# Three steps of a chunked linear-attention recurrence moved by one half group among the projection matmuls

## The reference, cut to what matters

```python
def step(carry, inp):                       # one chunk of tokens, all heads
    c_s, n_s, m = carry
    ...
    s = jnp.einsum('bhtd,bhsd->bhts', qc, kc) * jnp.exp(dmat - m_t[..., None])
    num = (w_inter[..., None] * jnp.einsum('bhtd,bhde->bhte', qc, c_s)
           + jnp.einsum('bhts,bhse->bhte', s, vc))
    ...
    h_out = num / jnp.maximum(jnp.abs(den), jnp.exp(-m_t))[..., None]
    ...
    c_new = decay[..., None, None] * c_s + jnp.einsum('bhs,bhsd,bhse->bhde', wk, kc, vc)
```

## Time and profile before

| what | us |
|---|---|
| median of 3 runs | 2176.84 (2175.14 to 2182.24) |
| the profiled execution, as timed | 2182.6 |
| its span in the trace | 2180.9 |
| late projections with the recurrence, in the trace | 119 to 367 |
| first matmuls after the barrier | from 369.79 |

### The profile page before, as it was taken

One profiled execution on the slowest core, in us unless ns is written; L12 is line 12 of the kernel. 1 busy time (PEld: TensorE's weight loads), 2 busy tenths in 40 slices (PEclk: granted clock), 3 DMA queues, 4 the chain that ended last, 5 costly groups with the idle time before them and its releaser, 6 DMA issues.

```text
span 2180.9 us, 39001 instructions
## 1 busy us (share of the span) xinstructions
PE 2104.2 (96%) x11205; PEld 1814.9 (83%) x11206; DVE 1597.7 (73%) x2121; ACT 1274.1 (58%) x1631; POOL 911.1 (42%) x909
## 2 busy tenths in 40 slices
PE   7999999999997999999999999999999999999996
PEld 6877777865886998888998899899887899889895
DVE  4555662553337778898878987888998888898876
ACT  4245342545235667676666766666776766776664
POOL 2015762244564234445334533433546443543532
PEclk9999998799996999999999999999999999999998
DMA  5233455303245779899877987987999987998976
GB/s 187 76 92 109 138 141 143 101 1 103 86 147 197 258 261 356 271 383 388 272 260 255 375 295 262 349 270 258 369 384 376 389 282 260 362 388 289 357 260 213
DMA packets 290264, 543.26 MB, mean 249 GB/s; under 512 B 39400, under 2 KB 51653, under 8 KB 290212
## 3 DMA queue, kind: packets, MB, share of 16 engines
q1 hardware_dynamic: 267972, 486.17, 66.1%
q0 software_dynamic: 22240, 56.42, 6.9%
HBM read 509.34 MB, written 44.14 MB: 254 GB/s over the span
## 4 chain that ended last, share of the span: by engine, by line
PE 75%; DVE 2%; DMA 2%; issue 2%; ACT 1%; POOL 0%; SPq 0%; DVEq 0%; POOLq 0%; ACTq 0%
PE banks L2634 17%; PE banks L208 11%; PE banks L210 11%; PE banks L209 11%; PE banks L2636 7%; PE banks L2011 3%; PE banks L2570 2%; PE banks L2569 2%; PE banks L1295 2%; DMA RAW<-in_expert_w_gate_up 1%; PE banks L2633 1%; PE banks L1997 1%; PE banks L1996 1%; DVE VL L1274 1%; PE banks L1973 1%
## 5 line engine op out<-in xcount | busy, mean ns | idle before, releaser
L1274 DVE TENSOR_TENSOR VL<-RAW,VH 128x2048 fp32r<-128x2048 f32 x389 | 882.2, 2287 | 28.8 <-ACT VH L1269 23.2
L1269 ACT ACTIVATE VH<-RAW 128x2048 fp32r<-128x2048 f32 x390 | 733.7, 1910 | 111.6 <-PE banks L210 76.3
L2634 PE MATMUL banks<-T,VH 128*128 128x384 f32 x1920 | 542.1, 357 | 2.5 <-DVE T L1315 2.5
L2636 PE MATMUL banks<-T,VL 128*128 128x192 f32 x1680 | 422.1, 251 | 0.0
L2634 PEld LDWEIGHTS banks<-T,VH 128*128 128x128 f32 x1920 | 345.8, 190 | 3.4 <-issue 2.9
L2636 PEld LDWEIGHTS banks<-T,VL 128*128 128x128 f32 x1680 | 321.6, 191 | 0.5
L2329 POOL DMA_INDIRECT out<-yb,ycur x32 | 78.3, 2447 | 413.0 <-DVE yb L2473 395.8
L209 PE MATMUL banks<-VL,T 128*128 128x512 f32 x544 | 211.9, 390 | 0.0
L208 PE MATMUL banks<-VH,T 128*128 128x512 f32 x544 | 211.9, 390 | 0.0
L210 PE MATMUL banks<-VH,T 128*128 128x512 f32 x544 | 211.8, 389 | 0.0
L208 PE MATMUL banks<-VH,A 128*128 128x512 f32 x512 | 204.1, 399 | 4.5 <-DVE A L2453 3.3
(11 more groups left out here) (391 smaller groups left out, 4070.1 us busy)
## 6 DMA issues: line engine op xcount, KB each, us to landing
RAW<-in_expert_w_gate_up SPq DMA_DIRECT2D x528, 512.0 KB
RAW<-in_expert_w_down SPq DMA_DIRECT2D x262, 512.0 KB
RW<-in_w_in SPq DMA_DIRECT2D x24, 512.0 KB, 5.8
xin<-in_x SPq DMA_DIRECT2D x8, 512.0 KB, 11.4
MBC<-dM SPq DMA_DIRECT2D x8, 512.0 KB, 11.1
dQ<-parts SPq DMA_DIRECT2D x8, 512.0 KB, 3.0
dK<-parts SPq DMA_DIRECT2D x8, 512.0 KB, 3.0
WRAW<-in_w_out SPq DMA_DIRECT2D x8, 512.0 KB, 8.3
```

The costliest lines, as they stand in the source:

```text
L1269: act.activation(VH[:, i, ks], RAW[:, i, ks], ACT.Copy).then_inc(s_hi, 1)
L1274: dve.tensor_tensor(VL[:, i, ks], RAW[:, i, ks], VH[:, i, ks].bitcast(f32), ALU.subtract).then_inc(s_w, 1)
L2634: last = pe.matmul(o[:, 0:2 * NW], VH[:, c % 3, k, col], T2[:, k], start=k == 0, stop=k == KT - 1)
L2636: pe.matmul(o[:, HI_ALL], VL[:, c % 3, k, col], T2[:, k, HI_ALL], start=False, stop=False)
```

## The change

On PE, `keys` goes from slot 1 to slot 0 and `update` from slot 5 to slot 6. On DVE, `quotient` goes from slot 6 to slot 5 and `state` from slot 5 to slot 6. ACT, POOL and SP keep their programs. No instruction is added or removed.

```diff
@@ DVE, piece
                         if s == 4:
                             numerator(t)
                         if s == 5:
+                            quotient(t)
+                        if s == 6:
                             state(t)
-                        if s == 6:
-                            quotient(t)
@@ PE, piece
                     elif t < TT:
-                        if s == 1:
+                        if s == 0:
                             keys(t)
                         if s == 2:
                             from_state(t)
                             scores(t)
                         if s == 4:
                             from_chunk(t)
-                        if s == 5:
+                        if s == 6:
                             update(t)
```

## The result

The changed kernel takes 2186.11 us (median of 12 runs, 2183.84 to 2191.68), the kernel before, timed beside it, 2180.63 (12 runs). The ratio is 1.003, 95% interval 1.0019 to 1.004: slower by 4.1 to 8.7 us; the medians differ by 5.5. Forecast were 7.6 us, 1.0035.

What follows compares the result with a forecast made beforehand. PE was taken to bound the kernel, with DVE's queue ahead of state now stopping it. Steps +6.0 us, quotient 0 and clock +1.6 gave +7.6 on 2176.84, so 2184.4 us, range 2176.5 to 2190.

Steps and rivals of the forecast that it cites:

- Step 0: Keys 0 wait 2.9 us for the gate factors; PE 0.4 us later at the state's read, lower end -1.4.
- Step 1: The numerator's wait of 1.84 us goes, keys 2 wait 1.4 us behind DVE's weight parts; net -0.5 us.
- Step 2: DVE's sums of group q3 stand ahead of the state, keys 3 wait 0.3 us; net +0.1 us.
- Step 3: Last group of q: state behind normed and two weight parts, keys 4 wait 8.6 us; +4.1 us, the dearest.
- Step 4: State behind the rest of k0, held by ACT's rounding and a store; keys 5 wait 3.3 us, net +1.8.
- the ruler: PE's stretch lengths from the earlier profile: half 2.72 us, update 0.90 more, keys to state's read 2.95, on to from_chunk 8.05.
- Step 5: State behind normed of k5, keys 6 wait 3.4 us, waits for v's weights (2.2) go; net -1.0 us.
- Step 6: State behind the rest of k7, held by a late store; keys 7 wait 2.9 us; net +1.1 us.
- The clock term: PE's stands of about 3 us bring one fall to half clock: +1.6 us, range 0 to 5.4.
- stores land on their own: Rival: late stores land soon after issue, so two DVE waits and the clock loss go; +0.1 us, 2176.9, chance 0.09.
- lost time is absorbed: Rival: DVE is the real pace and lost time is found again; +1 us, 2178, chance 0.07.
- worse: Rival: every PE stand brings half clock and two quotients are held 1.9 us each; +15.2 us, 2192.0, chance 0.08.

Runs made afterwards that it cites:

- c: Changed kernel, but DVE calls state in slot 5 right behind the quotient and stands there until PE's update; ratio to the kernel before 0.9996.
- a: Kernel before with only PE's keys moved from slot 1 to slot 0; ratio to the kernel before 1.0005.
- d: Changed kernel with DVE's quotient moved from slot 5 to slot 6, behind state; ratio to the kernel before 1.0055.
- e: Changed kernel with PE's keys back in slot 1 and DVE standing at state in slot 5; 2178.75 us against 2181.91 before, ratio 0.9975.
- f: Kernel before with DVE's first two weight parts ahead of normed in a projection's last group; ratio to the kernel before 0.9983.
- g: Kernel e with DVE's first two weight parts ahead of normed in a projection's last group; total ratio 0.998.

## Why the prediction was right, and where it was not

The mechanism held: c, which differs from the changed kernel only in what DVE has queued ahead of the state, gets all of the 7.9 us back, so half a group is enough in sum and the loss was the queue. By steps, each against the same place before, the stage's later start of 0.75 us taken off:

*Step 0.* Stand 2.58 (forecast 2.9), read of the state 0.6 later (0.4). Then the clock: 1.00 from 136 to 144, so by the next step PE was 1.1 ahead. I had taken the fall, and it did not come; my lower end, -1.4, was nearly met.

*Step 1.* Net -0.6 (-0.5), wait 0.97 (1.4). *Step 2.* +0.3 (+0.1).

*Step 3.* Wait 8.30 (8.6), `state` behind the two weight parts as forecast; net +3.4 (+4.1). From keys to read 7.19 us, of which 1.5 is the clock (2.1 forecast).

*Step 4.* Wait 2.96 (3.3). Net +3.3 instead of +1.8, because the clock fell: keys to read took 281.22 - 273.85 = 7.37 where the ruler says 5.67.

*Step 5.* Wait 3.71 (3.4). The waits for the weights of `v` went, as forecast, but to `from_chunk` 6 the net is +2.1 instead of -1.0: keys to read took 8.19, 2.5 of it clock.

*Step 6.* Wait 2.56 (2.9), no fall behind it, net +1.2 (+1.1). After it 0.6 came back where I had 0; 0.35 of it is a wait for the rows that attention's keys are turned from (tile KRAW, a load), which is gone.

The clock in three stretches of the changed kernel, behind steps 0, 5 and 6 (the eighth column):

```profile
136.00:144.00 8.00, 7.99 (x35) 6.22 (x35) 0.76 (x2) 7.86 (x20) 2.94 (x2) 1.00 0.22 70
...
302.00:309.00 7.00, 4.98 (x13) 4.04 (x14) 4.64 (x11) 1.06 (x1) 4.81 (x5) 0.53 0.40 112
330.00:340.00 10.00, 7.43 (x38) 6.02 (x37) 3.12 (x9) 3.98 (x10) 2.06 (x3) 1.00 0.66 254
```

So the six waits were sized within 0.5 us each, the steps without their clock within 0.6, and the sum of 7.6 met the measured 7.9 partly by luck. The clock term is the one that was wrong: it was +1.6 for one fall of at most 1.8, and two falls came, 1.7 + 2.5 = 4.2 us in steps 4 and 5. Against that step 0 gave back most of the 1.8 that I had left standing, and step 3 0.6. "A stand of 1.93 was followed by half clock, one of 1.84 by none" was no rule. In the changed kernel stands of 2.58 and 2.56 were followed by none, of 2.96 and 3.71 by one. The other runs show that the length does not decide at all: 2.58 in step 0 was followed by a fall in a and d (keys to read 7.25 and 7.20 us instead of 5.70), 1.93 and 1.90 in the two executions of e by none and by one, and 1.83 in f by one.

The signs of being right all came: the waits in front of L936, none for turned keys or numerator, and the first row behind the barrier 8.7 us later. Of the signs of being wrong one came too, the stage behind the barrier 4.3 us shorter, and the executions above show that one kernel does this by itself.

The rival in which stores land on their own is out: ACT's rounding of k0 and k7 was late as before, and DVE idled 4.35 and 5.33 us for it. The one in which lost time is absorbed is out too, only the waits for the weights of `v` were. The "worse" one had more half clock, which came, and held quotients, which did not. The quotient was never held for more than 0.9 us in slot 5 (the longest of its last parts 1.58 against 0.69, in step 3, ahead of a wait for POOL anyway), so 0 was right here; in c it cost 0.84.

## What to carry to other kernels

A distance between two slots must be compared with the whole queue of the engine between them, not with the duration of the one step: 3.42 us of work fitted into 3.62, and PE still stood 18.5 us. When a producer's step is moved behind work that itself waits for a third engine or a store, its consumer inherits that wait; letting the engine stand at the urgent step (c, e) was cheaper here than filling the gap, though the work that it pushed back cost 1.3 us elsewhere. Changing the order on one engine can come back through another: look at who is fed by the work that is pushed back, and who shares with it.

## What was not expected of the hardware

Behind the barrier one kernel (e) spent 42 us at a mean granted clock of 0.52 in one execution and 0.88 in another, and the stage took 174.02 and 163.03 us, 11 us of 2181. The Trainium skill, TensorE: Matmul & The Clock Gate, Part 1, says that one kernel can run a different number of slow matmuls from run to run, with the phase of the gate; the traces agree that it differs, with more time at stake than the whole effect of this change, and none shows the phase.

POOL and DVE held each other also with small operands. POOL's root on 128x8 values took 2.49 us beside DVE's weight parts instead of 1.64 (f); DVE's first instruction of the quotient, on 128x8 values too, took 1.63 us beside POOL's `exponents` instead of 0.15 (f); and a weight part took 2.29 to 2.89 us beside them instead of 1.21 (e, g).
